# A transpose of normalized keys: 8 TensorE transposes and a ScalarE copy per group, or 16 VectorE transposes of 32x32 squares

## The chip, the core and the metric

One NeuronCore of one Trainium2 chip runs the whole kernel; no other core takes part. The metric is the device time of one execution in microseconds (us), lower is better. The kernel before takes 1832.06 us, the median of 3 runs (1832.05 to 1832.18).

## What is computed

Four layers on 256 tokens of 2048 features, batch 1, all in fp32: a latent attention layer, an mLSTM layer, an HGRN2 layer, and a "forgetting attention" (FoX) layer of 16 heads of 128. The change is in the last one. Cut to what matters:

```python
def shared_kv(x, norm_w, w_kvf, f_bias, k_norm_w):
    h = rmsnorm(x, norm_w)
    kvf = h @ w_kvf                                   # 2048 -> 2048 keys, 2048 values, 16 forget gates
    k = kvf[..., :D_MODEL].reshape(B, T, FOX_HEADS, FOX_HDIM)
    ...
    k = head_rmsnorm(k, k_norm_w).transpose(0, 2, 1, 3)

def head_rmsnorm(x, w):
    return x * rsqrt(mean(x * x, axis=-1) + EPS) * w  # w: one weight for each of the 128 features of a head

def forgetting_attention(q, k, v, F):
    s = einsum('bhqd,bhkd->bhqk', q, k) * FOX_HDIM ** -0.5 + F[t] - F[s]
    # causal mask, softmax, times v
```

The keys come out of the projection with tokens on the partitions. The score product needs them with the 128 features of a head on the partitions, so every head's keys are transposed once.

## The kernel before

**Projections.** A weight matrix is streamed in units of 256 rows x 512 columns. Each fp32 unit is split into a high and a low part so that three fast products stand for an exact one. Three engines pass a unit on: SyncE's queue loads it into `wraw` (8 buffers); ScalarE makes the high part (`high`, line 270; the instruction is L283); VectorE makes the low part by a subtraction of 128x1024 (`low`, line 285; the instruction is L298); TensorE runs 12 matmuls of 128x512 on it (`products`, line 301; L365 to L367). The split parts have 4 buffers each (`SPLIT = 4`): ScalarE may split unit n only when TensorE has finished unit n-4, VectorE follows ScalarE, and TensorE waits for VectorE's semaphore `w_low`. The load of unit n waits until VectorE has split unit n-8.

**Order of the work.** It is written out by hand. Each engine walks the same list of units (a phase), and behind unit p each engine has the side work that belongs there. ScalarE and VectorE are `LAG = 3` units ahead of TensorE in that list: side work that reads a tile of products is put at `late(name, unit)`, which is that unit plus 3.

**The last layer.** Phase `l3_kv` runs 4 times (groups of 4 heads), with 16 units each: units 0 to 7 give 512 columns of keys, units 8 to 15 give 512 columns of values. Phase `l3_q` follows, also 4 times 16 units, with the queries and the output gate. A group's keys are evacuated into `qw3` (128 tokens x 2 blocks x 512) while the values are being computed, and they are handled in the next run of the phase (group 3 in the first run of `l3_q`): `kv_side(g, p)` exists on three engines.

- At p = 3 (`late("l3_kv", 0)`): ScalarE squares `qw3` into PSUM; VectorE sums by head (L2332), scales and adds eps (L2335); ScalarE takes the inverse root; VectorE multiplies both blocks by it (L2338, semaphore `kn`, `head_norm` at line 2329).
- At p = 5 on TensorE: it waits for `kn` and runs the 8 transposes of 128x128 of `turn_window` (L2798) from `qw3` into two PSUM banks, then raises `kt`.
- At p = 8 on ScalarE (`keys`, line 1507): it waits for `kt` and copies the 128x1024 from PSUM to `kT3` (L1511), scaling each feature (partition) by the key norm's weight, and raises `kT`.

The queries of group 0 wait for `kT` = 4 at line 2828. The evacuation of the next keys into `qw3` waits for `kt` (line 955). The queries use the same `turn_window` and are scaled by `sm[:, 56:57]` (the query norm's weight times 128 ** -0.5) when copied from PSUM. The last-layer loop of `l3_kv` is a hardware loop (`Fori`) on all engines.

Of the kernel before, what the change touches and what calls it, by code (L numbers as in the profile page):

```python
# [19 lines left out]
ALU = mybir.AluOpType  # L20
ACT = mybir.ActivationFunctionType
# [4 lines left out]
TB = T // P  # L26
# [20 lines left out]
H2, HD = 16, 128  # L47
# [37 lines left out]
def build(nc, a, out):  # L85

    with ExitStack() as ctx:
# [13 lines left out]
        colB = sb("colB", [P, NB_ROWS])  # L101
# [73 lines left out]
        def first(it):  # L175

            return isinstance(it, int) and it == 0
# [249 lines left out]
        def late(name, at):  # L427

            return min(at + LAG, length(name) - 1)
# [152 lines left out]
        def sems(layer, names):  # L582
            return {n: sem(f"l{layer}_{n}") for n in names.split()}
# [325 lines left out]
        def group(first, g, n=4):  # L909

            return slice(first + n * g, first + n * g + n) if isinstance(g, int) else bass.ds(first + n * g, n)
# [5 lines left out]
        def query_banks(p):  # L917
# [15 lines left out]

        l3 = sems(3, "r_dg r_row f_row f_e f_ok kss qss oss ksq kv_ krs kn kt kT qsq qv qrs qn qt qT sc msk mx ex pt ptc pv o "
                     "ge gs sq v rs on og ogp tmp hi lo")

        def dst_l3(name, k, b, it):
# [164 lines left out]
        def _(act):  # L1104
            own = Own(act, act_own)
            turn = Turn()
# [394 lines left out]
            def kv_side(g, p):  # L1501
                def norm():
                    landed(act, "l3_kv", 0, g)
                    squares(l3["ksq"], qw3)
                    inverse_root(l3["kv_"], l3["krs"], g)

                def keys():

                    act.wait_ge(l3["kt"], g + 1)
                    act.wait_ge(l3["f_ok"], 2)  # L1510
                    nc.scalar.activation(kT3[:, group(0, g), :].rearrange("p h t -> p (h t)"), ps2(0), ACT.Copy,  # L1511
                                         scale=colB[:, 80:81]).then_inc(l3["kT"], 1)
                if p == late("l3_kv", 0):
                    norm()
                if p == late("l3_kv", 5):
                    keys()

            for p in range(2, length("l3_kv")):
                step(act, high, evac, "l3_kv", p, 0, ("l3_f", 0))
# [93 lines left out]
        def _(dve):  # L1613
# [690 lines left out]
                    nc.vector.tensor_scalar(rdiag[:, b * P:(b + 1) * P], ident[:], nrm[:, b, 2:3], None,  # L2304
                                            ALU.mult).then_inc(l3["r_dg"], 1)

            own.mark(nc.vector.tensor_scalar(sm[:, 56:57], colB[:, 81:82], HD ** -0.5, None, ALU.mult))


            dve.wait_ge(l1["pads"], 2)  # L2310
# [18 lines left out]
            def head_norm(dst, src, sq, ss, vs, rs, on, g):  # L2329

                dve.wait_ge(sq, g + 1)
                nc.vector.tensor_reduce(sm[:, 32:40], ps2(2).rearrange("p (n d) -> p n d", d=HD), AX,  # L2332
                                        ALU.add).then_inc(ss, 1)
                dve.wait_ge(ss, g + 1)
                nc.vector.tensor_scalar(sm[:, 32:40], sm[:, 32:40], 1.0 / HD, EPS, ALU.mult, ALU.add).then_inc(vs, 1)  # L2335
                dve.wait_ge(rs, 2 * g + 2)
                for b in range(TB):
                    nc.vector.tensor_tensor(dst[:, b, :].rearrange("p (h d) -> p h d", d=HD),  # L2338
                                            src[:, b, :].rearrange("p (h d) -> p h d", d=HD),
                                            sm[:,  # L2340
                                               48 + 4 * b:52 + 4 * b].unsqueeze(2).to_broadcast([P, 4, HD]), ALU.mult).then_inc(on, 1)
# [7 lines left out]
            def kv_side(g, p):  # L2349
                if p == late("l3_kv", 0):  # L2350
                    head_norm(qw3, qw3, l3["ksq"], l3["kss"], l3["kv_"], l3["krs"], l3["kn"], g)

            for p in range(2, length("l3_kv")):
                step(dve, low, evac, "l3_kv", p, 0, ("l3_f", 0))
# [6 lines left out]
                for n in query_banks(p - LAG):  # L2361
                    b, q = n // 4, n % 4
                    d = (slice(4 * q, 4 * q + 4), slice(b * P, (b + 1) * P))
                    turn_dve(dve, turn, TBf[0][:, d[0], d[1]], TBf[1][:, d[0], d[1]], colB[:, 48 + 4 * q:52 + 4 * q])
            with dve.Fori(1, 4) as it:
                for p in range(length("l3_kv")):
                    step(dve, low, evac, "l3_kv", p, it, ("l3_kv", it - 1))
                    kv_side(it - 1, p)
# [82 lines left out]
        def _(pe):  # L2451
# [342 lines left out]
            def turn_window(done):  # L2794

                for h in range(4):
                    for b in range(TB):
                        m = nc.tensor.transpose(ps2(0)[:, h * T + b * P:h * T + (b + 1) * P],  # L2798
                                                qw3[:, b, h * HD:(h + 1) * HD], ident[:])
                m.then_inc(done, 1)  # L2800

            def kv_side(g, p):
                if p == 5:
                    pe.wait_ge(l3["kn"], 2 * g + 2)
                    pe.wait_ge(tr_lo, turn.n)
                    turn_window(l3["kt"])

            for p in range(length("l3_kv")):
                products(pe, "l3_kv", p, in_src)
                for n in query_banks(p):  # L2810
# [6 lines left out]
            with pe.Fori(1, 4) as it:  # L2817
                for p in range(length("l3_kv")):
                    products(pe, "l3_kv", p, in_src, it)
                    kv_side(it - 1, p)  # L2820

            def q_src(k, q):
                return TBf[0], TBf[1], q
# [1 line left out]
            def q_side(g, u):  # L2825
                def queries():
                    pe.wait_ge(l3["qn"], 2 * g + 2)
                    pe.wait_ge(l3["kT"], 4)
                    if g > 0:
                        pe.wait_ge(l3["lo"], 2 * g)  # L2830
                    turn_window(l3["qt"])

                def scores(hh):
                    pe.wait_ge(l3["qT"], g + 1)
                    pe.wait_ge(l3["f_ok"], 3)
                    fox.scores(pe, g, hh)
                    fox.scores(pe, g, hh + 1)

                def back():
                    pe.wait_ge(l3["og"], g + 1)  # L2840
                    pe.wait_ge(l3["msk"], 4 * g + 4)
                    for b in range(TB):
                        for i in range(4):
                            m = nc.tensor.transpose(ps[:, b, i * P:(i + 1) * P], o3[:, b, i * P:(i + 1) * P], ident[:])
                        m.then_inc(l3["ogp"], 1)

                if u == L3_AT["turn"]:
                    queries()
                if u == L3_AT["sc0"]:
                    scores(0)  # L2850
                if u == L3_AT["t0"]:
                    fox.turn(pe, g, 0)
                if u == L3_AT["v0"]:
                    fox.values(pe, g, 0)
                    fox.turn(pe, g, 1)
                if u == L3_AT["v1"]:
                    fox.values(pe, g, 1)
                    scores(2)
                if u == L3_AT["t2"]:
                    fox.turn(pe, g, 2)  # L2860
                if u == L3_AT["v2"]:
                    fox.values(pe, g, 2)
                    fox.turn(pe, g, 3)
                if u == L3_AT["v3"]:
                    fox.values(pe, g, 3)
                if u == L3_AT["back"]:
                    back()

            pe.wait_ge(tr_lo, turn.n)
            for p in range(length("l3_q")):  # L2870
                products(pe, "l3_q", p, q_src)
                kv_side(3, p)
                q_side(0, p)
            for it in range(1, 4):
                for p in range(length("l3_q")):
# [35 lines left out]
```

## Time and profile before

| | |
|---|---|
| median of 3 runs | 1832.06 us |
| profiled execution, span from first to last instruction | 1830.5 us |
| TensorE matmuls busy | 1816.5 us, 99% of the span |
| VectorE busy | 1262.5 us, 69% |
| ScalarE busy | 946.6 us, 52% |
| DMA engines, mean throughput | 174 GB/s |
| phase `l3_kv` and first run of `l3_q` | about 1340 to 1570 us |

The profiled execution has no time of its own beside the span in what was recorded; its span is 1.56 us below the median of the runs, which is what lies around the first and last instruction. Busy times of matmuls overlap by design (a matmul is listed with 0.39 us and the next starts 0.23 us later), so starts are compared, not lengths. VectorE's records overlap in the same way where nothing is waited for. An entry "x2" in a timeline is a merged pair: its length runs from the first start to the last end. The number in brackets is the idle time of the engine before the entry, and what ended it.

### The profile page before, as it was taken

What the parts mean: (1) busy time and instruction counts of PE and PEld (TensorE: products, weight loads), DVE (VectorE), ACT (ScalarE), POOL (GpSimd) and SP (SyncE); (2) the same over time, 40 slices, a digit from 0 to 9 for tenths busy, and PEclk for the clock granted to TensorE, in tenths of its full rate; (3) what the DMA queues carried; (4) which work ended last, traced back from release to release, by engine and by line L of the source; (5) the groups of instructions that cost most, each with busy time, mean ns of one, the idle gap of its engine ahead of it and who ended that gap; (6) DMA issues with size and microseconds to landing.
All of it is one profiled execution on the core that took longest, in us unless ns stands there. A gap on an engine that the chain in (4) does not pass through costs nothing.

```text
span 1830.5 us, 24740 instructions
## 1 busy us (share of the span) xinstructions
PE 1816.5 (99%) x9031; PEld 1533.8 (84%) x9031; DVE 1262.5 (69%) x1703; ACT 946.6 (52%) x1314; POOL 37.8 (2%) x116
## 2 busy tenths in 40 slices
PE   8999999999999999999999999999999999999999
PEld 7899998788888888887888888888888888888887
DVE  6676766588556755767887868787776555577764
ACT  4545554455465545536554555555435444565542
POOL 2000000000000004000000000000000000000000
PEclk9999999999999999999999999999999999999999
DMA  8555454668889887565655555545546666555453
GB/s 293 162 177 148 139 177 154 203 177 185 183 150 213 178 180 167 198 239 151 181 175 159 156 175 156 181 149 170 178 138 206 185 192 186 161 156 166 154 168 115
DMA packets 170029, 319.41 MB, mean 174 GB/s; under 512 B 16264, under 2 KB 20768, under 8 KB 169168
## 3 DMA queue, kind: packets, MB, share of 16 engines
q1 hardware_dynamic: 168800, 313.69, 60.2%
q10 hardware_dynamic: 576, 4.19, 0.6%
q8 instruction: 61, 1.00, 0.2%
q0 software_dynamic: 560, 0.26, 0.1%
q14 instruction: 32, 0.26, 0.0%
HBM read 316.01 MB, written 2.10 MB: 174 GB/s over the span
## 4 chain that ended last, share of the span: by engine, by line
PE 97%; DVE 2%; ACT 1%; issue 0%; DMA 0%; DVEq 0%; ACTq 0%
PE acc L365 27%; PE acc L367 27%; PE acc L366 27%; PE ps L614 2%; PE ps L2712 2%; PE ps L462 1%; DVE wlo L298 1%; PE acc L331 1%; PE acc L332 1%; PE acc L330 1%; PE ps L647 1%; PE acc L348 0%; PE acc L354 0%; PE acc L352 0%; PE acc L349 0%
## 5 line engine op out<-in xcount | busy, mean ns | idle before, releaser
L298 DVE TENSOR_TENSOR wlo<-wraw,whi 128x1024 fp32r<-128x1024 f32 x579 | 699.5, 1222 | 345.1 <-ACT whi L283 342.5
L283 ACT ACTIVATE whi<-wraw 128x1024 fp32r<-128x1024 f32 x579 | 599.8, 1052 | 355.2 <-PE acc L367 322.9
L365 PE MATMUL acc<-whi,ta_hi 128*128 128x512 f32 x1664 | 660.4, 397 | 4.5 <-DVE wlo L298 2.4
L367 PE MATMUL acc<-whi,ta_lo 128*128 128x512 f32 x1664 | 649.7, 390 | 0.0
L366 PE MATMUL acc<-wlo,ta_hi 128*128 128x512 f32 x1664 | 648.3, 390 | 0.0
L365 PEld LDWEIGHTS acc<-whi,ta_hi 128*128 128x128 f32 x1664 | 312.7, 188 | 69.6 <-issue 3.9
L367 PEld LDWEIGHTS acc<-whi,ta_lo 128*128 128x128 f32 x1664 | 312.4, 188 | 66.6
L366 PEld LDWEIGHTS acc<-wlo,ta_hi 128*128 128x128 f32 x1664 | 313.0, 188 | 62.0
L365 PE MATMUL acc<-whi,tb_hi 128*128 128x512 f32 x576 | 228.6, 397 | 0.1
L367 PE MATMUL acc<-whi,tb_lo 128*128 128x512 f32 x576 | 225.0, 391 | 0.0
L366 PE MATMUL acc<-wlo,tb_hi 128*128 128x512 f32 x576 | 224.5, 390 | 0.0
L367 PEld LDWEIGHTS acc<-whi,tb_lo 128*128 128x128 f32 x576 | 108.1, 188 | 23.0
L365 PEld LDWEIGHTS acc<-whi,tb_hi 128*128 128x128 f32 x576 | 108.3, 188 | 22.2 <-DVE wlo L298 0.7
L366 PEld LDWEIGHTS acc<-wlo,tb_hi 128*128 128x128 f32 x576 | 108.3, 188 | 21.2
L1421 ACT ACTIVATE arena<-arena 128x512 f32<-128x512 f32 x64 | 37.6, 637 | 83.5 <-DVE arena L2159 72.5
L638 ACT ACTIVATE arena<-arena,sm 128x128 f32<-128x128 f32 x64 | 28.7, 449 | 54.9 <-DVE sm L628 53.9
L404 ACT ACTIVATE arena<-acc 128x512 f32<-128x512 f32 (+2 forms) x41 | 23.3, 568 | 35.1 <-PE acc L367 25.2
L614 PE MATMUL ps<-arena 128*128 128x128 f32 (+1 forms) x192 | 36.8, 331 | 0.0
L1130 ACT ACTIVATE arena<-acc,nrm 128x512 f32<-128x512 f32 (+1 forms) x32 | 21.8, 680 | 28.3 <-PE acc L367 27.1
L2712 PEld LDWEIGHTS ps<-arena 128*128 128x128 f32 x256 | 33.5, 191 | 2.7
L475 ACT ACTIVATE tb_hi<-tmpT 128x512 fp32r<-128x512 f32 x20 | 12.6, 632 | 43.5 <-DVE tmpT L484 43.5
L2159 DVE TENSOR_TENSOR arena<-arena 128x1024 f32<-128x1024 f32 x28 | 33.9, 1212 | 0.1
(325 smaller groups left out, 1650.2 us busy)
## 6 DMA issues: line engine op xcount, KB each, us to landing
wraw<-in_ml_w_in SPq DMA_DIRECT2D x129, 512.0 KB, 6.1
wraw<-in_a_w_in SPq DMA_DIRECT2D x128, 512.0 KB, 3.9
wraw<-in_kv_w SPq DMA_DIRECT2D x64, 512.0 KB, 3.7
wraw<-in_b_w_in SPq DMA_DIRECT2D x64, 512.0 KB, 4.3
wraw<-in_mla_w_in SPq DMA_DIRECT2D x49, 512.0 KB, 4.9
wraw<-in_mla_w_out SPq DMA_DIRECT2D x32, 512.0 KB, 3.8
wraw<-in_ml_w_out SPq DMA_DIRECT2D x32, 512.0 KB, 4.6
wraw<-in_a_w_out SPq DMA_DIRECT2D x32, 512.0 KB, 4.0
```

The lines of the kernel that those rows point to most:

```text
L283: nc.scalar.activation(unit_of(whi, n, SPLIT, w), unit_of(wraw, n, RAW, w), ACT.Copy).then_inc(w_high, 1)
L298: nc.vector.tensor_tensor(unit_of(wlo, n, SPLIT, w), unit_of(wraw, n, RAW, w), unit_of(whi, n, SPLIT, w).bitcast(F32), ALU.subtract).then_ ...
L365: nc.tensor.matmul(o, xh, wh, start=first, stop=False)
L366: nc.tensor.matmul(o, xh, wl, start=False, stop=False)
L367: m = nc.tensor.matmul(o, xl, wh, start=False, stop=end)
L404: nc.scalar.activation(dst, result(name, k, 0, dst.shape[0]), ACT.Copy).then_inc(out_b0, 1)
L614: m = nc.tensor.matmul(o, x, y, start=i == 0, stop=i == len(parts) - 1)
L638: nc.scalar.activation(v, v, ACT.Exp, bias=sm[:, 2 * w + b:2 * w + b + 1], accum_out=sm[:, 4 + 2 * w + b:5 + 2 * w + b]).then_inc(self.l[" ...
L1130: nc.scalar.activation(DST(name, k, 0, it, act), result(name, k, 0, P), ACT.Copy, scale=nrm[:, 0, 2:3]).then_inc(out_b0, 1)
L1421: nc.scalar.activation(d[:, :, c, :], d[:, :, c, :], ACT.Exp, scale=1.0 if c and j else -1.0).then_inc(l2["ee"], 1)
L2159: nc.vector.tensor_tensor(d, b, b[:, :, :, h:h + 1].to_broadcast([P, 8, 64 // h, 2 * h]), ALU.subtract).then_inc(l2["df"], 1)
L2712: m = nc.tensor.matmul(ps[:, 2 + j % 2, o], kx[:, j % 2, o], qx[:, j % 2, o], start=True, stop=True)
```

## The change

The last layer's keys are no longer transposed by TensorE and copied by ScalarE. VectorE, straight behind its two multiplications at p = 3, issues 16 `transpose` instructions per group. Each reads 32 partitions (tokens 32i to 32i+31 of both blocks, features 32j to 32j+31 of the four heads, 256 columns) and writes the transposed 32x32 squares to partitions 32j to 32j+31 of `kT3`. i is the outer loop, j the inner. The last of them raises `kt`. The key norm's weight is folded into the query's scale instead (features are on the partitions there too, so the product of both weights does it). TensorE's wait for the keys moves to the scores. VectorE's loop over runs 1 to 3 of `l3_kv` is written out in the program instead of a hardware loop.

```diff
-        l3 = sems(3, "... ksq kv_ krs kn kt kT qsq ...
+        l3 = sems(3, "... ksq kv_ krs kn kt qsq ...
...
         # ScalarE, kv_side
-                def keys():
-
-                    act.wait_ge(l3["kt"], g + 1)
-                    act.wait_ge(l3["f_ok"], 2)
-                    nc.scalar.activation(kT3[:, group(0, g), :].rearrange("p h t -> p (h t)"), ps2(0), ACT.Copy,
-                                         scale=colB[:, 80:81]).then_inc(l3["kT"], 1)
                 if p == late("l3_kv", 0):
                     norm()
-                if p == late("l3_kv", 5):
-                    keys()
...
         # VectorE
-            own.mark(nc.vector.tensor_scalar(sm[:, 56:57], colB[:, 81:82], HD ** -0.5, None, ALU.mult))
+            own.mark(nc.vector.tensor_scalar(sm[:, 56:57], colB[:, 81:82], HD ** -0.5, colB[:, 80:81], ALU.mult,
+                                             ALU.mult))
...
             def kv_side(g, p):
                 if p == late("l3_kv", 0):
                     head_norm(qw3, qw3, l3["ksq"], l3["kss"], l3["kv_"], l3["krs"], l3["kn"], g)
+                    if not first(g):
+                        dve.wait_ge(l3["f_ok"], 2)
+                    keys = kT3[:, group(0, g), :].rearrange("p h (b i c) -> p i b h c", b=TB, i=4)
+                    dve.wait_ge(l3["kn"], 2 * g + TB)
+                    for i in range(4):
+                        rows = qw3[32 * i:32 * i + 32, :, :].rearrange("q b (h j c) -> q j b h c", h=4, j=4)
+                        for j in range(4):
+                            m = nc.vector.transpose(keys[32 * j:32 * j + 32, i], rows[:, j])
+                    m.then_inc(l3["kt"], 1)
...
-            with dve.Fori(1, 4) as it:
+            for it in range(1, 4):
                 for p in range(length("l3_kv")):
                     step(dve, low, evac, "l3_kv", p, it, ("l3_kv", it - 1))
                     kv_side(it - 1, p)
...
         # TensorE
-            def kv_side(g, p):
-                if p == 5:
-                    pe.wait_ge(l3["kn"], 2 * g + 2)
-                    pe.wait_ge(tr_lo, turn.n)
-                    turn_window(l3["kt"])
...
                     products(pe, "l3_kv", p, in_src, it)
-                    kv_side(it - 1, p)
...
                 def queries():
                     pe.wait_ge(l3["qn"], 2 * g + 2)
-                    pe.wait_ge(l3["kT"], 4)
+                    pe.wait_ge(l3["f_ok"], 2)
...
                 def scores(hh):
                     pe.wait_ge(l3["qT"], g + 1)
                     pe.wait_ge(l3["f_ok"], 3)
+                    pe.wait_ge(l3["kt"], 4)
...
                 products(pe, "l3_q", p, q_src)
-                kv_side(3, p)
                 q_side(0, p)
```

## Rows read from the trace of the kernel before

**Rows 1.** The page: busy time, TensorE clock in slices, chain that ended last.

```profile
PE 1816.5 (99%) x9031; PEld 1533.8 (84%) x9031; DVE 1262.5 (69%) x1703; ACT 946.6 (52%) x1314; POOL 37.8 (2%) x116
...
PEclk9999999999999999999999999999999999999999
...
PE 97%; DVE 2%; ACT 1%; issue 0%; DMA 0%; DVEq 0%; ACTq 0%
```

**Rows 2.** Waits of PE's weight loads, 1340 to 1545 us: total, times, longest.

```profile
PEld acc L365 <- DVE wlo L298: 0.4, 1, 0.4
```

**Rows 3.** Timeline of PE: start us, length us, engine, line, operation.

```profile
1403.29 0.39 PE L365 MATMUL acc<-whi,ta_hi 128*128 128x512 f32 x1
...
1408.50 0.39 PE L367 MATMUL acc<-whi,ta_lo 128*128 128x512 f32 x1
1408.73 1.04 PE L2798 MATMUL ps<-ident,arena 128*128 128x128 f32 x8
1409.52 0.48 PE L365 MATMUL acc<-whi,ta_hi 128*128 128x512 f32 x1
1409.84 0.39 PE L366 MATMUL acc<-wlo,ta_hi 128*128 128x512 f32 x1
```

**Rows 4.** Timeline of PE, the next group and the last one.

```profile
1453.16 1.03 PE L2798 MATMUL ps<-ident,arena 128*128 128x128 f32 x8
...
1542.01 1.03 PE L2798 MATMUL ps<-ident,arena 128*128 128x128 f32 x8
```

**Rows 5.** Timeline of VectorE in the first of the four groups.

```profile
1397.47 1.29 DVE L2338 TENSOR_TENSOR arena<-arena,sm 128x512 f32<-128x512 f32 x2 [0.52 <-ACT sm L1499]
1398.68 2.36 DVE L298 TENSOR_TENSOR wlo<-wraw,whi 128x1024 fp32r<-128x1024 f32 x2
1401.86 1.23 DVE L298 TENSOR_TENSOR wlo<-wraw,whi 128x1024 fp32r<-128x1024 f32 x1 [0.83 <-ACT whi L283]
...
1412.01 1.22 DVE L298 TENSOR_TENSOR wlo<-wraw,whi 128x1024 fp32r<-128x1024 f32 x1 [3.48 <-ACT whi L283]
```

**Rows 6.** Timeline of VectorE: catching up before the groups, second group, fourth group.

```profile
1382.51 4.61 DVE L298 TENSOR_TENSOR wlo<-wraw,whi 128x1024 fp32r<-128x1024 f32 x4
...
1443.10 2.35 DVE L298 TENSOR_TENSOR wlo<-wraw,whi 128x1024 fp32r<-128x1024 f32 x2
...
1531.85 2.35 DVE L298 TENSOR_TENSOR wlo<-wraw,whi 128x1024 fp32r<-128x1024 f32 x2
```

**Rows 7.** Timeline of VectorE in layer 0, moves between quarters of the partitions.

```profile
82.72 0.41 DVE L1790 TENSOR_TENSOR arena<-arena 32x256 f32<-32x256 f32 x1
83.17 0.42 DVE L1791 TENSOR_TENSOR arena<-arena 32x256 f32<-32x256 f32 x1
```

**Rows 8.** Timeline of VectorE, other instructions of 256 columns.

```profile
48.14 0.29 DVE L1653 TENSOR_SCALAR arena<-arena 128x256 f32<-128x256 f32 x1
48.35 1.22 DVE L298 TENSOR_TENSOR wlo<-wraw,whi 128x1024 fp32r<-128x1024 f32 x1
...
406.87 0.74 DVE L1985 TENSOR_SCALAR arena<-arena,colA 128x256 f32<-128x256 f32 x2 [2.28 <-ACT arena L1280]
...
1381.59 0.68 DVE L2325 TENSOR_TENSOR_SCAN arena<-ones,arena 16x256 f32<-16x256 f32 x1
1382.30 0.28 DVE L2327 COPY ones<-arena 16x256 f32<-16x256 f32 x1
```

**Rows 9.** Timeline of VectorE and of PE at the first split of weights.

```profile
11.23 4.87 DVE L298 TENSOR_TENSOR wlo<-wraw,whi 128x1024 fp32r<-128x1024 f32 x4 [0.25 <-ACT whi L283]
...
5.97 5.72 PE L462 MATMUL ps<-ident,x_res 128*128 128x128 f32 x32 [5.97 <-DMA x_res<-in_x]
...
12.60 0.47 PE L365 MATMUL acc<-whi,ta_hi 128*128 128x512 f32 x1 [0.91 <-DVE wlo L298]
```

**Rows 10.** Stretches: PE, PEld, DVE, ACT, POOL busy, then granted clock, DMA share, GB/s.

```profile
0.00:5.00 5.00, 0.00 (x0) 0.00 (x0) 0.00 (x0) 1.28 (x1) 3.61 (x48) 1.00 0.57 197
1390.00:1413.00 23.00, 23.00 (x107) 19.15 (x106) 12.75 (x13) 11.51 (x14) 0.00 (x0) 1.00 0.66 202
```

More of the change, by code:

```diff
@@ L932, in build @@
         rdiag = kT3[:, 13, :]
-        l3 = sems(3, "r_dg r_row f_row f_e f_ok kss qss oss ksq kv_ krs kn kt kT qsq qv qrs qn qt qT sc msk mx ex pt ptc pv o "
+        l3 = sems(3, "r_dg r_row f_row f_e f_ok kss qss oss ksq kv_ krs kn kt qsq qv qrs qn qt qT sc msk mx ex pt ptc pv o "
                      "ge gs sq v rs on og ogp tmp hi lo")
```

## The prediction, made before the change was run

> **What bounds the kernel now.** I read the page first. TensorE's matmuls are busy for 99% of the span, the chain that ended last is 97% TensorE, and the granted clock is in its top tenth in every slice [rows 1]. So time is TensorE's time, and another engine counts only where TensorE waits for it. The second view was the waits of the stretch that changes: in 205 us of the last layer TensorE's weight loads waited for VectorE's split once, 0.4 us [rows 2]. The stretch is packed: work taken off TensorE is gained at its full price, and a VectorE that is late is paid in full once its lead is used up. The third view, the timelines of TensorE and VectorE around the removed transposes, gives that lead [rows 3 to 6].
>
> **What is removed from TensorE.** The 8 transposes start at 1408.73 and the next unit's first matmul at 1409.52 [rows 3]. The better price is the period of a whole run of the phase: the same transposes start 44.43 us later in the next group [rows 3, 4]. In that period lie 16 units of 12 matmuls. Starts from 1403.29 to 1408.50 are 23 matmuls apart, 0.2265 us each [rows 3]; 192 of them make 43.5 us. The transposes cost 44.43 - 43.5 = 0.91 us per group, 3.64 us for four. That is the whole possible gain, 0.20% of the time.
>
> **What is removed from ScalarE.** A copy of 128x1024 per group and the wait for TensorE ahead of it. While that copy stood in ScalarE's queue, VectorE sat idle for 3.48 us waiting for the next split [rows 5], and TensorE still did not wait [rows 2]. It was covered by the lead, so taking it away gains nothing.
>
> **What is added to VectorE, and the spacing of one instruction.** 16 instructions of 32 partitions x 256 columns per group. No transpose of VectorE is in this trace. The nearest rows are the moves of layer 0: also 32 partitions, also 256 columns of fp32, also read in one quarter of the partitions and written to another. They take 0.41 us, and the next starts 0.45 us after the first, with no wait between them in the program [rows 7]. Other instructions of 256 columns are closer together: a pair on all partitions with 0.74 us for both has a spacing of about 0.74 - 0.41 = 0.33 us, and a one-input instruction of 0.29 us let the next one start after 0.21 us [rows 8]. The far end above is an instruction that takes two cycles or so for a column, the scan of 256 columns: 0.68 us, and the next starts 0.71 us behind it [rows 8]. I take 0.45 us, since those rows share the shape and the crossing of quarters. Ends: 0.21 and 0.71.
>
> The Trainium skill ("VectorE: DVE Perf Modes", section "Two Vector instructions with no wait between them") says why crossing rows would be further apart: an instruction whose output starts in another quarter than the last output starts only when all earlier ones have finished. All 16 of the change do this, since j is the inner loop. Rows 7 agree with it (0.45 with a crossing, against 0.33 without one in rows 8). Without the rule one could take 0.33, and the sum below would give +5.0 us in place of +12.6. The same page (section "The three transpose paths") lists 311 ns for a VectorE transpose of 128 columns of bf16; with 0.13 us for 128 more columns and the 0.035 us gap of rows 7 this would be an estimate of 0.48 us of spacing, and +14.5 us. No row here shows either figure.
>
> **What is queued behind it.** This is the heart of the change. The multiplications end at 1397.47 + 1.29 = 1398.76, and behind them on VectorE stands the split of unit 4, then 5, 6, 7. Before, the split of unit 4 started at 1398.68 and ended about 1399.90 (one of the pair of 2.36 us) [rows 5]. TensorE began unit 4 at 1403.29 [rows 3]; it is 24 matmuls, so 5.44 us, ahead of the transposes, which follow unit 5. The lead is 3.39 us. In the new order the burst starts about 1398.80, and the split of unit 4 starts at 1398.80 + 16 x 0.45 = 1406.00, ends at 1407.22, and TensorE can start some 0.15 us later (11.23 + 1.22 = 12.45 against 12.60 at the first split) [rows 9]: 1407.37. The wait of TensorE is 1407.37 - 1403.29 = 4.08 us. In general it is 16 x spacing - 3.12 us.
>
> Does it repeat within the group? Units 5 to 7 are ready for VectorE by then, and it catches up at 1.15 us a unit (four in 4.61 us [rows 6]) while TensorE takes 2.72 us. So it is one wait per group. The second group has the same lead: split at 1443.10, transposes at 1453.16, so 1447.72 - 1444.32 = 3.40 us [rows 4, 6]; the third repeats it. The fourth, in `l3_q`: 1542.01 - 5.44 = 1536.57 against 1531.85 + 1.22 = 1533.07, a lead of 3.50 us [rows 4, 6], so a wait of 3.97 us.
>
> **Edits that I cost at nothing.** The folded scale is one instruction on one column in either kernel. The loads: SyncE's queue waits for the split of unit n-8, so it is held for 7.2 us, but 8 raw units cover 8 x 2.72 = 21.8 us of TensorE; if that cover were gone, every us of delay would be one of TensorE. `kt` for the next evacuation into `qw3` now comes at 1406 and is needed behind unit 10's split, some 10 us later; it was raised at about 1409.8 before. The scores of group 0 wait for four `kt`, long past. The queries drop the wait for `kT`. The written-out loop removes loop registers from VectorE only, where there is slack, and adds program text; no wait of rows 2 is tied to the loop.
>
> **The sum.** Waits: 3 x 4.08 + 3.97 = 16.2 us. Gain: 3.6 us. Net +12.6 us on the profiled span of 1830.5 us; the runs' median is 1.56 us above that span, and I carry that over: 1832.06 + 12.6 = **1844.6 us**, 0.7% slower. A measurement of this kernel can tell about 0.2%, 3.7 us, from no change.
>
> **Rivals.**
> 1. *The instructions lie as close as those on all partitions* (0.33 us): wait 2.16 us per group less 0.91, +5.0 us, 1837.1 us. For it: the pair of rows 8. Against it: rows 7. Chance 0.11.
> 2. *The burst is hidden: not slower.* The place is the lead of 3.4 us behind the multiplications. It decides by the spacing: at (3.12 + 0.91)/16 = 0.25 us gain and wait balance, and below it the kernel gets faster. With the one-input spacing of 0.21 us [rows 8] the wait is 0.24 us, the net -0.67 us per group, 1829.4 us; with no wait at all 1828.4 us. For it: a transpose has one input, as that instruction. Against it: the crossing of quarters, which made a gap behind every instruction in rows 7. Chance 0.08.
> 3. *The clock falls in the new waits.* The waits of 4 us would be the longest of TensorE behind its start. Nowhere here is the clock below its upper level of 2.4 GHz, not in the stretch [rows 10], nor right after the idle 5.97 us at the start [rows 9, 10], but no wait of this length in mid-work is in the trace. If one unit per wait ran at 1.2 GHz, it would take 5.44 us in place of 2.72, four times: +10.9 us on top, 1855.5 us; in one or two of the groups, 1847 to 1850. The Trainium skill ("TensorE: Matmul & The Clock Gate", section "Why this matters for your kernels") warns of gaps of about this length in mid-work, after which the clock is halved; the trace neither agrees nor contradicts. Chance 0.12.
> 4. *A transpose of fp32 takes about two cycles a column*, like the scan (0.71 us): wait 8.24 us, less 0.91, four times, 1861.4 us. Only the scan speaks for it. Chance 0.07.
> 5. *It does not do what it says*: the builder cuts each instruction into its 8 squares or VectorE is slowed otherwise; over 1862 us. Chance 0.02.
>
> **How the numbers follow.** The forecast has 0.60. Its own range, spacings 0.42 to 0.50 us, is 1842.7 to 1847.8 us. The range for 8 in 10 takes the forecast, most of rival 3 and the upper half of the cases between 0.33 and 0.45: 1837 to 1856 us; left out are rivals 2, 4, 5 and a little of 1. Faster by over 0.2% is below 1828.4 us, which even the full gain only touches: 0.02. Within 0.2% (to 1835.7 us) is rival 2 with a bit of rival 1: 0.07. Slower: 0.91.
>
> **What would show it.** In the changed kernel: 64 transposes on VectorE with starts 0.45 us apart, 7.2 us per group; the split of unit 4 starting about 7.3 us behind the end of the multiplications; four waits of about 4.1 us of L365 for L298, at about 1403, then each 48 us or so later (44.43 + 3.2), the last in `l3_q`; the transposes of L2798 halved from 64 to 32; ScalarE's L1511 gone, with VectorE's 3.48 us idle time. The step that carries all is the spacing: waits near 2 us mean rival 1, none rival 2, over 8 us rival 4. I am also wrong if the waits come out as said but the granted clock is below 1 behind them, or if TensorE waits a second time in the same group, so that a delayed unit pulls others with it.

## The result, and the profile after it

| | before | after |
|---|---|---|
| median | 1832.05 us (1831.96 to 1832.18, 4 runs) | 1853.84 us (1851.68 to 1854.31, 4 runs) |
| ratio | | 1.0117, 95% interval 1.0105 to 1.0128 |
| profiled execution: its time, its span | span 1830.5 us | 1854.15 us, span 1852.4 us |
| mean granted clock | 1.000 | 0.994 |

The change makes the kernel 21.8 us slower. The forecast was 12.6 us. The wide range of 1837 to 1856 us holds the result, since it was drawn to take in most of rival 3; the forecast's own range of 1842.7 to 1847.8 us misses it by 6 us. The waits came as worked out; the lower clock behind them, a rival with a chance of 0.12, came too, in all four groups.

The page of the changed kernel: busy times, clock in slices, chain, and the group of the first matmul of each unit's triple (behind the second bar: idle time of the engine ahead of it, and what ended it).

```profile
PE 1823.0 (98%) x8999; PEld 1536.3 (83%) x8999; DVE 1290.6 (70%) x1767; ACT 942.9 (51%) x1310; POOL 37.8 (2%) x116
...
PEclk9999999999999999999999999999999999999999
...
PE 95%; DVE 3%; ACT 1%; issue 1%; DMA 0%; DVEq 0%; ACTq 0%
...
L365 PE MATMUL acc<-whi,ta_hi 128*128 128x512 f32 x1664 | 663.1, 398 | 16.2 <-DVE wlo L298 14.2
...
L365 PE MATMUL acc<-whi,tb_hi 128*128 128x512 f32 x576 | 229.5, 399 | 3.8 <-DVE wlo L298 3.8
```

The first of these two groups on the page of the kernel before:

```profile
L365 PE MATMUL acc<-whi,ta_hi 128*128 128x512 f32 x1664 | 660.4, 397 | 4.5 <-DVE wlo L298 2.4
```

Against [rows 1] hardly anything moves: 99% to 98%, 97% to 95%, and the clock's digits stay 9 because a slice is 46 us. This page would not give the cause away. What speaks is the idle time ahead of L365 that VectorE's split ended: 14.2 us where it was 2.4 us, and 3.8 us more in the group that reads `tb_hi`, where the kernel before had none. That is 15.6 us of new idle time, spread over the four groups of heads.

The waits of the stretch (total, times, longest), to be set against the one of 0.4 us in [rows 2]:

```profile
PEld acc L365 <- DVE wlo L298: 17.6, 5, 4.3
PE acc L365 <- DVE wlo L298: 15.5, 4, 3.9
```

The second line counts matmuls: four new waits of 3.8 to 3.9 us. The first counts weight loads, which wait the same four times, and once more for the old 0.4 us. VectorE in the first group, as in [rows 5]:

```profile
1397.23 1.29 DVE L2331 TENSOR_TENSOR arena<-arena,sm 128x512 f32<-128x512 f32 x2 [0.52 <-ACT sm L1499]
1398.56 7.19 DVE L2352 STREAM_TRANSPOSE arena<-arena 32x256 f32<-32x256 f32 x16
1405.77 4.63 DVE L298 TENSOR_TENSOR wlo<-wraw,whi 128x1024 fp32r<-128x1024 f32 x4
1413.55 1.23 DVE L298 TENSOR_TENSOR wlo<-wraw,whi 128x1024 fp32r<-128x1024 f32 x1 [3.15 <-ACT whi L283]
```

The 16 transposes stand between the multiplications and the split of unit 4, which moved from 1398.68 to 1405.77. Behind it VectorE catches up with four splits in a row. The instruction itself, over all 64 (min/median/max ns):

```profile
L2352 DVE STREAM_TRANSPOSE arena<-arena x64: 432/436/441, 1398.6 to 1555.2; 32x256 f32<-32x256 f32 x64
```

16 of them take 7.19 us from first start to last end, so the next starts 0.45 us after the last: (7.19 - 0.43)/15. TensorE in the same group, as in [rows 3]:

```profile
1402.82 0.39 PE L367 MATMUL acc<-whi,ta_lo 128*128 128x512 f32 x1
1407.05 0.79 PE L365 MATMUL acc<-whi,ta_hi 128*128 128x512 f32 x1 [3.84 <-DVE wlo L298]
1407.64 0.63 PE L366 MATMUL acc<-wlo,ta_hi 128*128 128x512 f32 x1
1408.07 0.63 PE L367 MATMUL acc<-whi,ta_lo 128*128 128x512 f32 x1
...
1411.91 0.51 PE L367 MATMUL acc<-whi,ta_lo 128*128 128x512 f32 x1
1412.26 0.40 PE L365 MATMUL acc<-whi,ta_hi 128*128 128x512 f32 x1
1412.49 0.39 PE L366 MATMUL acc<-wlo,ta_hi 128*128 128x512 f32 x1
```

Two losses are seen here. Between 1402.82 and 1407.05 TensorE has nothing to do. And then its matmuls are 0.427 us apart (0.59 us behind the very first), not 0.227, until 1412.26. The stretches of this group, with the columns of [rows 10] (the granted clock is the figure behind POOL's):

```profile
1395.00:1405.00 10.00, 8.21 (x37) 6.46 (x35) 9.22 (x20) 4.46 (x7) 0.00 (x0) 1.00 0.19 59
1405.00:1412.40 7.40, 5.35 (x13) 4.25 (x14) 5.36 (x6) 0.00 (x0) 0.00 (x0) 0.54 0.53 165
1412.40:1420.00 7.60, 7.60 (x36) 6.26 (x35) 3.45 (x3) 3.18 (x3) 0.00 (x0) 1.00 0.70 219
```

The clock is 1.00 ahead of it, 0.54 over the rest of the wait and the slow matmuls, 1.00 behind. At 0.54 most of the stretch is at 1.2 GHz, the lower of the two levels. In the other three groups the first matmul behind the wait and the first one at full speed again are:

```profile
1457.15 0.79 PE L365 MATMUL acc<-whi,ta_hi 128*128 128x512 f32 x1 [3.91 <-DVE wlo L298]
...
1463.55 0.40 PE L365 MATMUL acc<-whi,ta_hi 128*128 128x512 f32 x1
...
1507.77 0.79 PE L365 MATMUL acc<-whi,ta_hi 128*128 128x512 f32 x1 [3.92 <-DVE wlo L298]
...
1511.26 0.39 PE L367 MATMUL acc<-whi,ta_lo 128*128 128x512 f32 x1
...
1556.97 0.79 PE L365 MATMUL acc<-whi,tb_hi 128*128 128x512 f32 x1 [3.81 <-DVE wlo L298]
...
1562.54 0.39 PE L366 MATMUL acc<-wlo,tb_hi 128*128 128x512 f32 x1
```

From these the whole difference can be added up. A wait is the idle time plus 0.16 us, since a matmul is listed 0.39 us long while the next may start after 0.227. A slow stretch is its length less what its matmuls take at 0.227 us.

| group | wait | slow matmuls | time lost by them |
|---|---|---|---|
| 1 | 3.84 + 0.16 = 4.00 us | 12 | 5.21 - 2.72 = 2.49 us |
| 2 | 3.91 + 0.16 = 4.07 us | 15 | 6.40 - 3.40 = 3.00 us |
| 3 | 3.92 + 0.16 = 4.08 us | 8 | 3.49 - 1.81 = 1.68 us |
| 4 | 3.81 + 0.16 = 3.97 us | 13 | 5.57 - 2.95 = 2.62 us |
| sum | 16.1 us | 48 | 9.8 us |

16.1 + 9.8 - 3.6 of transposes taken off TensorE = 22.3 us; the spans differ by 21.9 us (1852.4 - 1830.5), and TensorE reached unit 4 of the first group 0.24 us earlier than before (1402.82 + 0.23 = 1403.05 against 1403.29). Not all of the 9.8 us is the clock's: the next matmul behind the first one after a wait starts late even where the clock stays up (0.34 us in place of 0.227 in experiment 1 below, 1407.02 to 1407.36), which with the slightly wide spacings after it is about 0.14 us a group, 0.5 to 0.6 us in all. That leaves 9.2 us for the clock.

### The profile page after: what moved, and what is told of

Read it like the earlier page. It is cut to its first block, busy times and chain, and to the rows that moved or that the text cites. A ratio compares the mean times of both kernels' runs of the same rounds, so it can differ in the third digit from the quotient of the medians.

```text
span 1852.4 us, 24665 instructions
## 1 busy us (share of the span) xinstructions
PE 1823.0 (98%) x8999; PEld 1536.3 (83%) x8999; DVE 1290.6 (70%) x1767; ACT 942.9 (51%) x1310; POOL 37.8 (2%) x116
## 4 chain that ended last, share of the span: by engine, by line
PE 95%; DVE 3%; ACT 1%; issue 1%; DMA 0%; DVEq 0%; ACTq 0%
PE acc L365 27%; PE acc L367 27%; PE acc L366 27%; PE ps L614 2%; PE ps L2714 2%; DVE arena L2352 1%; PE ps L462 1%; DVE wlo L298 1%; PE acc L331 1%; PE acc L332 1%; PE acc L330 1%; PE ps L647 1%; ACT whi L283 1%; PE acc L348 0%; PE acc L349 0%
## 5 line engine op out<-in xcount | busy, mean ns | idle before, releaser
L365 PE MATMUL acc<-whi,ta_hi 128*128 128x512 f32 x1664 | 663.1, 398 | 16.2 <-DVE wlo L298 14.2
L365 PEld LDWEIGHTS acc<-whi,ta_hi 128*128 128x128 f32 x1664 | 314.3, 189 | 83.2 <-DVE wlo L298 13.9
L365 PE MATMUL acc<-whi,tb_hi 128*128 128x512 f32 x576 | 229.5, 399 | 3.8 <-DVE wlo L298 3.8
L365 PEld LDWEIGHTS acc<-whi,tb_hi 128*128 128x128 f32 x576 | 108.9, 189 | 26.4 <-DVE wlo L298 4.8
L1130 ACT ACTIVATE arena<-acc,nrm 128x512 f32<-128x512 f32 (+1 forms) x32 | 21.8, 682 | 28.4 <-PE acc L367 27.2
L475 ACT ACTIVATE tb_hi<-tmpT 128x512 fp32r<-128x512 f32 x20 | 12.6, 632 | 43.5 <-DVE tmpT L484 43.5
```

Of the source, the lines that this page charges most:

```text
L365: nc.tensor.matmul(o, xh, wh, start=first, stop=False)
L1130: nc.scalar.activation(DST(name, k, 0, it, act), result(name, k, 0, P), ACT.Copy, scale=nrm[:, 0, 2:3]).then_inc(out_b0, 1)
```

## The experiments

The theory at this point: the place of the block costs 16.1 us of waiting, the waiting brings the lower clock and 9.8 us more, and the removed transposes give 3.6 us back. The times stand against the kernel before on the same chip, 1832.09 us for the first four and 1832.14 us for the next four.

**1. Fill the wait with matmuls that nobody needs.** This keeps the waits and takes away only TensorE's idleness.

```diff
+            def fill():
+                for _ in range(16):
+                    nc.tensor.matmul(ps[:, 0, :], TA[0][:, 0, 0:P], TA[0][:, 0:2, :].rearrange("p k t -> p (k t)"),
+                                     start=True, stop=True)
...
+                    if p == 4:
+                        fill()
                     products(pe, "l3_kv", p, in_src, it)
...
+                if p == 4:
+                    fill()
                 products(pe, "l3_q", p, q_src)
```

> The changed kernel, with 16 matmuls of 128x512 that nothing reads put into TensorE's queue ahead of unit 4 in the four places where it waits 4.0 us for the split; they take 16 x 0.227 = 3.6 us of that wait, so 0.4 us of waiting is left and no work is delayed by them. Theory (the half-clock stretches behind the waits come from TensorE having nothing to do): the matmuls of unit 4 and 5 run at 0.227 us spacing, granted clock 1.00 throughout, and the 9.8 us of slow matmuls go: before + 16.1 of waits - 3.6 of transposes = 1844.5 us. Rival (the matmuls are slow because VectorE's catching up or its transposes take something from TensorE): the 0.43 us spacing stays behind the wait, 1853 to 1854 us.

Measured: 1844.99 us (1844.83 to 1845.19), ratio 1.0071, interval 1.0054 to 1.0088. TensorE's timeline in the first group, and the stretch with its clock:

```profile
1402.79 0.39 PE L367 MATMUL acc<-whi,ta_lo 128*128 128x512 f32 x1
1403.02 3.79 PE L2806 MATMUL ps<-ta_hi 128*128 128x512 f32 x16
1407.02 0.50 PE L365 MATMUL acc<-whi,ta_hi 128*128 128x512 f32 x1 [0.22 <-DVE wlo L298]
1407.36 0.39 PE L366 MATMUL acc<-wlo,ta_hi 128*128 128x512 f32 x1
```

```profile
1402.00:1412.00 10.00, 9.78 (x44) 7.78 (x43) 9.07 (x14) 2.12 (x2) 0.00 (x0) 1.00 0.37 116
```

The split arrives at the same time as in the changed kernel (first matmul at 1407.02 against 1407.05), but the matmuls run at full speed at once, and the clock is 1.00. 8.9 us are gone from the median, 9.2 us from the profiled span (1852.4 - 1843.2), though TensorE got more work. So the slow matmuls come from the idleness, not from what VectorE does meanwhile. What is left is the forecast's own sum: 1844.6 us predicted, 1845.0 measured.

**2. Move the block behind the split of unit 7.**

```diff
             def kv_side(g, p):
                 if p == late("l3_kv", 0):
                     head_norm(qw3, qw3, l3["ksq"], l3["kss"], l3["kv_"], l3["krs"], l3["kn"], g)
+                if p == 7:
                     if not first(g):
                         dve.wait_ge(l3["f_ok"], 2)
```

> The changed kernel with its 16 transposes moved as one block from behind the multiplications (behind the split of unit 3) to behind the split of unit 7. Theory (the cost is where the block stands: behind the multiplications the lead is 3.4 us, four units later it is back at about 5.6 us, and 1.5 us of idle time of VectorE lie there too): a wait of about 0.2 us per group, no fall of the clock, -3.6 us of TensorE's transposes, 1829 us (1828.4 to 1831). Rival (VectorE cannot hold 7.2 us per group wherever they are; the lead is spent anyway): waits of 2 us or more per group, above 1838 us.

Measured: 1829.25 us (1829.02 to 1829.34), ratio 0.9984, interval 0.9975 to 0.9994. VectorE's timeline, and the waits of TensorE's weight loads:

```profile
1405.65 7.18 DVE L2353 STREAM_TRANSPOSE arena<-arena 32x256 f32<-32x256 f32 x16
1412.86 3.50 DVE L298 TENSOR_TENSOR wlo<-wraw,whi 128x1024 fp32r<-128x1024 f32 x3
```

```profile
PEld acc L365 <- DVE wlo L298: 1.3, 4, 0.4
```

The same 7.2 us block, on the same engine, in the same group: 24.6 us less than the change (1853.84 - 1829.25). One of the four waits is the old one of 0.4 us; the other three are new, 0.3 us each and of weight loads only. No matmul of the stretch waits for VectorE's split. The rival that VectorE cannot carry the work anywhere falls.

**3. Cut it in four blocks, behind the splits of units 3 to 6.**

```diff
-                    for i in range(4):
-                        rows = ...
-                        for j in range(4):
-                            m = nc.vector.transpose(keys[32 * j:32 * j + 32, i], rows[:, j])
-                    m.then_inc(l3["kt"], 1)
+                if 3 <= p < 7:
...
+                    i = p - 3
+                    rows = qw3[32 * i:32 * i + 32, :, :].rearrange("q b (h j c) -> q j b h c", h=4, j=4)
+                    for j in range(4):
+                        m = nc.vector.transpose(keys[32 * j:32 * j + 32, i], rows[:, j])
+                    if i == 3:
+                        m.then_inc(l3["kt"], 1)
```

> The changed kernel with the 16 transposes cut in four blocks of 4, behind the splits of units 3 (and the multiplications), 4, 5 and 6. Each block is 1.8 us; with the 1.15 us split it makes 2.95 us a unit against 2.72 of TensorE, so the lead falls from 3.4 by 1.8 and then by 0.2 a unit, to about 1 us at the least. Theory: TensorE does not wait at all, clock 1.00, 1832.05 - 3.6 = 1828.4 us, the whole gain. Rival (as in the block moved late): waits that add up, 1832 us or more.

Measured: 1829.03 us (1828.69 to 1829.17), ratio 0.9983, interval 0.9973 to 0.9993. Nearly the whole gain, but not quite "does not wait at all": one new wait was left, in the last group (0.8 us of a weight load, 0.4 us of the matmul behind it), where VectorE has three more instructions (for the bias rows) behind unit 6.

**4. Transposes that stay in their quarter.** The keys come out in another order; the rest is computed as before.

```diff
-                    for i in range(4):
-                        rows = qw3[32 * i:32 * i + 32, :, :].rearrange("q b (h j c) -> q j b h c", h=4, j=4)
-                        for j in range(4):
-                            m = nc.vector.transpose(keys[32 * j:32 * j + 32, i], rows[:, j])
+                    for j in range(4):
+                        rows = qw3[32 * j:32 * j + 32, :, :].rearrange("q b (h i c) -> q i b h c", h=4, i=4)
+                        for i in range(4):
+                            m = nc.vector.transpose(keys[32 * j:32 * j + 32, i], rows[:, i])
```

> The changed kernel with the same 16 transposes of 32x256 at the same place, but each reads and writes the same quarter of the partitions (quarter j to quarter j, four in a row per quarter), so the squares are turned but not moved between the quarters: the keys are in the wrong order, everything else is computed as before. Theory (the 0.45 us spacing comes from an instruction held back because its quarter is not the last one's): 12 of 16 spacings fall to about 0.35 us, 4 stay at 0.45; the block is 6.0 us, the wait 2.9 us per group, in sum -3.6 + 11.6 = +8 us, 1840 us with the clock up and 1846 to 1850 us if it falls behind waits of 2.9 us too. Rival (0.45 us is what a transpose takes at any place): spacing 0.45, waits 4.0 us, 1853 to 1854 us as the change.

Measured: 1845.39 us (1843.73 to 1845.68), ratio 1.0070, interval 1.0053 to 1.0087. All 64 transposes, and TensorE behind the first wait:

```profile
L2352 DVE STREAM_TRANSPOSE arena<-arena x64: 390/394/443, 1398.8 to 1547.7; 32x256 f32<-32x256 f32 x64
```

```profile
1405.80 0.50 PE L365 MATMUL acc<-whi,ta_hi 128*128 128x512 f32 x1 [2.37 <-DVE wlo L298]
...
1407.10 0.63 PE L367 MATMUL acc<-whi,ta_lo 128*128 128x512 f32 x1
...
1410.08 0.56 PE L365 MATMUL acc<-whi,ta_hi 128*128 128x512 f32 x1
```

The starts of the first group's 16 run from 1398.8 to 1404.1, so the mean spacing is 0.35 us, against 0.45. The law gives 16 x 0.35 - 3.12 = 2.5 us; measured 2.37 + 0.16. Changing the quarter therefore costs 0.1 us per instruction, 1.5 us for a group's block (7.19 us against 5.7). The clock fell in all four groups here too, a little later: from 1405.80 to 1407.10 five matmuls started at about full speed, and only then came the spacing of 0.43 us. The waits sum to 10.2 us; the span rose by 13.5 us, so with 3.6 us given back, 6.9 us belong to the slow matmuls.

**5. Exchange the two loops.**

```diff
-                    for i in range(4):
-                        rows = qw3[32 * i:32 * i + 32, :, :].rearrange("q b (h j c) -> q j b h c", h=4, j=4)
-                        for j in range(4):
+                    for j in range(4):
+                        for i in range(4):
+                            rows = qw3[32 * i:32 * i + 32, :, :].rearrange("q b (h j c) -> q j b h c", h=4, j=4)
                             m = nc.vector.transpose(keys[32 * j:32 * j + 32, i], rows[:, j])
```

> The changed kernel with the two loops around the 16 transposes exchanged: j (the quarter written) is outer, i (the quarter read) inner, so that four in a row write the same quarter and only the quarter read changes. The same 16 instructions, the same result. The Trainium skill's rule holds an instruction for either side, so by it nothing changes: spacing 0.45 us, 16 transposes in 7.2 us, 1852 to 1854 us. Rival (only the written quarter counts): 12 of 16 spacings at 0.35 us, block about 5.8 us, 1844 to 1847 us, like the run whose transposes stay in their quarter.

Measured: one run, 1854.17 us. VectorE's timeline in the first group:

```profile
1398.55 7.18 DVE L2352 STREAM_TRANSPOSE arena<-arena 32x256 f32<-32x256 f32 x16
1405.76 4.63 DVE L298 TENSOR_TENSOR wlo<-wraw,whi 128x1024 fp32r<-128x1024 f32 x4
```

7.18 us for 16, as before the exchange. A change of the quarter that is read alone spaces the instructions as far apart as a change of the quarter that is written alone. Any two of these 16 instructions differ in one or the other, so no order of the 16 in a row should be cheaper; orders other than these two were not run.

**6. The written-out loop alone**, on the kernel before.

```diff
-            with dve.Fori(1, 4) as it:
+            for it in range(1, 4):
                 for p in range(length("l3_kv")):
                     step(dve, low, evac, "l3_kv", p, it, ("l3_kv", it - 1))
```

> The kernel before with one edit of the change alone: VectorE's hardware loop over runs 1 to 3 of the keys' phase written out. Theory (costed at nothing in the prediction, since VectorE's lead covers it): 1832.05 us within 0.2 us, no new wait of TensorE. Rival (the longer program text or the loop's registers cost or save something that TensorE feels): a difference of 0.5 us or more.

Measured: 1832.11 us (1831.85 to 1832.69, 10 runs), ratio 1.0000, interval 0.9991 to 1.0010. The waits of the weight loads are those of [rows 2]:

```profile
PEld acc L365 <- DVE wlo L298: 0.4, 1, 0.4
```

It costs nothing that these runs can tell (0.03 us under the 1832.14 us of the kernel before on the same chip), as it was costed.

**7. A part of the block stays, the rest goes behind unit 7.** With 10 and with 12 of the 16 behind the multiplications:

```diff
+                if p in (3, 7):
...
-                    for i in range(4):
+                    for n in range(0 if p == 3 else 10, 10 if p == 3 else 16):    # or 12 for 10
+                        i, j = n // 4, n % 4
                         rows = qw3[32 * i:32 * i + 32, :, :].rearrange("q b (h j c) -> q j b h c", h=4, j=4)
-                        for j in range(4):
-                            m = nc.vector.transpose(keys[32 * j:32 * j + 32, i], rows[:, j])
-                    m.then_inc(l3["kt"], 1)
+                        m = nc.vector.transpose(keys[32 * j:32 * j + 32, i], rows[:, j])
+                    if p == 7:
+                        m.then_inc(l3["kt"], 1)
```

> The changed kernel with 10 of the 16 transposes behind the multiplications and the other 6 behind the split of unit 7. The law 16 x spacing - 3.12 us becomes 10 x 0.45 - 3.12 = 1.4 us of wait per group (1.3 in the last), 5.4 us in four; less 3.6 us of transposes: 1833.9 us if the clock stays up, as behind every shorter wait seen so far. If waits of 1.4 us already bring the lower clock: 1840 us or more. Rival to the law itself (the wait goes with the sum of VectorE's work and not with what stands between the multiplications and the next split): the wait stays at 4 us.

Measured with 10: 1834.10 us (1833.96 to 1834.25), ratio 1.0011, interval 1.0001 to 1.0021. The waits of the matmuls:

```profile
PE acc L365 <- DVE wlo L298: 4.6, 4, 1.2
```

4.6 + 4 x 0.16 = 5.2 us against 5.4 by the law; the clock stayed at 1.00. The time is 0.2 us from the 1833.9 expected. The rival to the law, a wait that stays at 4 us, falls: the same 16 instructions in the same group, six of them later, give a wait of 1.3 us.

> The changed kernel with 12 of the 16 transposes behind the multiplications and 4 behind the split of unit 7. Law: 12 x 0.45 - 3.12 = 2.28 us of wait per group (2.2 in the last), 9.0 us in four, less 3.6: 1837.5 us with the clock up. Behind waits of 1.4 us it stayed up, behind waits of 2.5 us it fell in all four groups; if it falls here too, some 1.7 us per group come on top, 1844 us; between the two if it falls in some groups only. Rival to the law: as for 10 of 16, a wait that does not go by 0.45 us per instruction.

Measured with 12: 1843.23 us (1842.40 to 1844.34), ratio 1.0060, interval 1.0043 to 1.0076, against 1832.20 us. TensorE behind the wait in the first and in the last group:

```profile
1405.26 0.79 PE L365 MATMUL acc<-whi,ta_hi 128*128 128x512 f32 x1 [2.03 <-DVE wlo L298]
1405.85 0.63 PE L366 MATMUL acc<-wlo,ta_hi 128*128 128x512 f32 x1
...
1547.65 0.50 PE L365 MATMUL acc<-whi,tb_hi 128*128 128x512 f32 x1 [1.98 <-DVE wlo L298]
...
1548.74 0.63 PE L366 MATMUL acc<-wlo,tb_hi 128*128 128x512 f32 x1
```

The waits are 2.1 to 2.3 us (2.03 + 0.16 in the first group; the law said 2.28), and the clock fell in all four groups. Two more instructions per group lengthened the waits by 0.9 us each, 3.6 us in all, and cost 9.1 us. In the first group the very first matmul behind the wait is slow, in the last one the slow ones begin about 1 us later (0.50 at 1547.65, then 0.63 from 1548.74).

**8. Four blocks behind the splits of units 6 to 9.** As experiment 3, with `6 <= p < 10` and `i = p - 6`.

> The changed kernel with the 16 transposes in four blocks of 4 behind the splits of units 6 to 9, where the lead is back at 5.6 us. Theory: the lead never falls under 3 us, no wait of TensorE in the four groups, 1828.4 to 1829.0 us, as good as blocks behind units 3 to 6 or 0.3 us better. Rival (ScalarE's evacuation at unit 10 waits for the last block and delays its next splits): waits behind unit 10, 1830 us or more.

Measured: 1828.37 us (1828.28 to 1828.50, 10 runs), ratio 0.9979, interval 0.9970 to 0.9989. VectorE's timeline in the first group, and the waits:

```profile
1401.78 1.23 DVE L298 TENSOR_TENSOR wlo<-wraw,whi 128x1024 fp32r<-128x1024 f32 x1 [0.83 <-ACT whi L283]
1402.92 1.77 DVE L2353 STREAM_TRANSPOSE arena<-arena 32x256 f32<-32x256 f32 x4
1404.71 1.23 DVE L298 TENSOR_TENSOR wlo<-wraw,whi 128x1024 fp32r<-128x1024 f32 x1
1405.97 1.78 DVE L2353 STREAM_TRANSPOSE arena<-arena 32x256 f32<-32x256 f32 x4
```

```profile
PEld acc L365 <- DVE wlo L298: 0.4, 1, 0.4
```

This is the best version: 3.8 us faster than the kernel before on the same chip and 25.5 us faster than the change, with the same instructions. The single wait left is the old one of 0.4 us. The rival (ScalarE's evacuation held up by the last block) did not show.

## Why the prediction was right, and where it was not

**Spacing of the transposes: right.** 0.45 us was taken from the moves of layer 0 [rows 7] and measured 0.45; the median instruction took 0.436 us where those took 0.41 to 0.42. The closer spacing of [rows 8], 0.33 us (rival 1), was the wrong choice for instructions that change quarters; it is near the 0.35 us of those that mostly stay in theirs (experiment 4). The Trainium skill's rule on held instructions ("VectorE: DVE Perf Modes", section "Two Vector instructions with no wait between them") was borne out twice: 0.35 us on average where 12 of 16 keep both quarters, 0.45 us with either side changed. The estimate of 0.48 us from that page's transpose figure was 0.03 us too high.

**The lead and the law of the wait: right.** 16 x 0.45 - 3.12 = 4.08 us was forecast, 4.00 to 4.08 us measured; in the last group 3.97 and 3.97. It also held for 10 and 12 instructions (1.3 and 2.2 us for 1.38 and 2.28) and for the closer spacing (2.5 us). One wait per group, as said.

**The gain on TensorE: right.** 3.64 us forecast; the version without any new wait gains 3.8 us. (With the spacing of 0.2265 us that the prediction names, its 44.43 - 43.5 is 0.93 us a group, 3.7 us in all; its 0.91 does not follow from the numbers shown.)

**The edits costed at nothing: right.** The written-out loop was tested by itself. That the copy of ScalarE, the loads and the semaphores cost nothing is borne out by experiment 8, which has all of these edits, no new wait and the full gain; they were not tested one by one. One sign of the prediction was off: with ScalarE's copy gone, VectorE's idle time of 3.48 us was to go too, but 3.15 us stand at 1413.55 in the changed kernel. There ScalarE, and VectorE behind it, wait for the late TensorE and not for a copy; in experiment 8, where TensorE is not late, no idle time of VectorE in this group is over 1.5 us.

**The clock: the step that failed.** The forecast kept the clock at its upper level ("Nowhere here is the clock below its upper level") and put its fall at 0.12. It fell behind every one of the four waits; the matmuls behind them lost 9.8 us, 1.7 to 3.0 us a group. With it rival 3's own figure, 10.9 us on top for 1855.5 us, comes close to the 1853.84 measured: its mechanism was right, and it should have been the forecast. That its size came out is in part luck: nothing in the trace before said that one unit, 12 matmuls, would run slowly behind each wait. It was 12 on average, but 8 to 15 in the single groups.

The trace before was also misread. The prediction says that the clock is at its upper level right after the 5.97 us of idle time at the start. But [rows 10] gives only the granted clock of a stretch in which TensorE did nothing, and [rows 9] merges the 32 transposes behind it into one entry. Taken apart, with the same shape in mid-work as the third line:

```profile
6.63 1.70 PE L462 MATMUL ps<-ident,x_res 128*128 128x128 f32 x7
...
L462 PE MATMUL ps<-ident,x_res x7: 421/421/422, 6.6 to 7.9; 128*128 128x128 f32 x7
...
L2798 PE MATMUL ps<-ident,arena x64: 269/273/294, 1408.7 to 1722.8; 128*128 128x128 f32 x64
...
9.76 0.93 PE L462 MATMUL ps<-ident,x_res 128*128 128x128 f32 x7
```

At 6.63 us seven transposes start (1.70 - 0.42)/6 = 0.213 us apart, at 9.76 us (0.93 - 0.27)/6 = 0.11 us apart, with no wait between them. The pace nearly doubles within TensorE's first work, as it does where the clock comes back behind the waits above (0.427 to 0.227). The granted clock is printed as 1.00 for both stretches, so that column does not show it and the pace is the evidence; the DMA share is near 1 in both (0.95 and 1.06), so it does not tell the two apart. The longest idle time of TensorE in the trace was therefore followed by some 3.5 us at about half pace (the last transposes 0.42 us long start at 9.4 us), and it spoke for rival 3, not against it.

The Trainium skill ("TensorE: Matmul & The Clock Gate", section "Why this matters for your kernels") warned of gaps in mid-work, and the trace agrees with it: experiment 1 took the idleness away and the fall with it. The gaps need not be as long as the 4 us of the change: the clock fell behind waits of 2.1 to 2.5 us as well. A rule that names the very event, with a trace whose first microseconds bear it out, deserved more than one part in eight.

**The other rivals.** The block was not hidden (rival 2), since 0.45 us lies far above the 0.25 us at which it would turn; it is hidden, however, in four blocks that start three units later (experiment 8), which the prediction did not look for. A transpose took 0.436 us, not the 0.68 us of the scan (rival 4), and 64 of them ran, not eight times as many (rival 5).

## What to carry to other kernels

An engine with 31% of idle time still has places where it has none to lend: read the lead (when its output is ready against when it is used) at the very place where work is added, and put the work where the lead is longest, in blocks that the lead covers. When the arithmetic gives a wait of TensorE of a few microseconds in mid-work, add a stretch at the lower clock behind it: here four waits of 4 us brought 10 us more, four of 2.2 us nearly 7, and four of 1.3 us nothing. If such a wait can't be removed, matmuls that nobody reads can give the clock's part back (experiment 1). And look at the first microseconds of a trace one instruction at a time: they can show both paces of TensorE.

## What was not expected of the hardware

- The clock fell behind every wait of 2.1 us or more (16 of 16, four each in the change, experiments 4 and 5, and experiment 7 with 12) and behind none of 1.3 us (4 of 4, experiment 7 with 10). Nothing between 1.3 and 2.1 us was measured. The price is not in proportion to the wait: 9.8 us for 16.1 us of waits, 6.9 us for 10.2, and for 12 of 16 it is 11.8 - 8.8 + 3.6 = 6.6 us for 8.8 us (11.8 us is the difference of the spans, 1842.3 - 1830.5). Within the change itself, waits of 4.07 and 4.08 us were followed by losses of 3.00 and 1.68 us.
- The fall can come after work has begun again: in experiment 4 about five matmuls (1.3 us) ran at full speed behind the first wait before the spacing went to 0.43 us. In the change it comes while TensorE still waits: the very first matmul is slow there.
- A matmul of 128x512 that is 0.227 us behind the last at the upper level is 0.427 us behind it at the lower, a little less than double.
- The number of slow matmuls varied from 8 to 15 between groups of one execution, and the runs of kernels whose clock falls scatter more: 1851.68 to 1854.31 us, against 1828.28 to 1828.50 for the best version. What sets the number was not tested.
